# A state-space scan over single positions becomes a scan over blocks of four, with factors made during the feed-forward ahead

## The reference

```python
lam_bar = jnp.exp(lam * dt)                       # 32 groups x 64 complex states
b_bar = ((lam_bar - 1.0) / lam)[:, :, None] * b_mat
bu = jnp.einsum('bsgh,gph->bsgp', uf.astype(jnp.complex64), b_bar)
_, states = lax.associative_scan(combine, (a, bu), axis=1)   # s[t] = lam_bar s[t-1] + bu[t]
y = jnp.real(jnp.einsum('bsgp,ghp->bsgh', states, c_mat))
y = y + uf * d_skip
y = jax.nn.gelu(y) ; y = y * sigmoid(y @ w_glu + b_glu)
```

## Time and profile before

| what | value |
| --- | --- |
| median of three runs | 3577.52 us |
| the profiled execution | 3578.64 us, of it the span 3576.8 us |
| TensorE busy | 3240.0 us, 91% |
| VectorE busy | 1843.5 us, 52% |
| ScalarE busy | 956.0 us, 27% |
| GpSimd busy | 380.7 us, 11% |
| mean granted TensorE clock | 0.945 |

### The profile page before, as it was taken

How to read it: one execution, slowest core, us unless ns; L and a number is a source line. 1 busy time by engine, 2 the same in 40 slices (tenths; PEclk the granted TensorE clock), 3 DMA queues, 4 the chain that set the end, 5 groups by cost and what they waited for, 6 DMA issues and landing times.

```text
span 3576.8 us, 49265 instructions
## 1 busy us (share of the span) xinstructions
PE 3240.0 (91%) x20420; PEld 2597.6 (73%) x20420; DVE 1843.5 (52%) x3234; ACT 956.0 (27%) x1669; POOL 380.7 (11%) x539
## 2 busy tenths in 40 slices
PE   8888899999999988899999999899997657789997
PEld 6556788999999866688887888678884212458886
DVE  2352476457564144257646846443335897453334
ACT  2444222232222144422223222222222001432122
POOL 1020121000000002012100000000000684000000
PEclk9999899999999999999999999999998766899999
DMA  5101011224342201011123534122221000112222
GB/s 184 65 13 42 31 60 53 73 101 165 142 142 95 93 36 36 30 45 60 60 91 119 186 121 161 64 89 94 94 100 42 18 0 0 36 61 103 90 99 72
DMA packets 69445, 283.24 MB, mean 79 GB/s; under 512 B 10297, under 2 KB 10681, under 8 KB 64233
## 3 DMA queue, kind: packets, MB, share of 16 engines
q1 hardware_dynamic: 57880, 230.04, 18.1%
q0 software_dynamic: 11344, 50.07, 3.9%
...
## 4 chain that ended last, share of the span: by engine, by line
PE 83%; DVE 11%; issue 3%; ACT 2%; POOL 1%; DMA 0%; DVEq 0%; ACTq 0%; SPq 0%; POOLq 0%
PE acc L1017 15%; PE acc L1018 15%; PE acc L1019 15%; PE acc L1032 8%; PE acc L1240 5%; PE acc L1241 4%; PE acc L1242 4%; PE acc L1179 3%; PE acc L1283 2%; PE acc L1124 2%; PE acc L1183 2%; PE acc L1097 1%; PE acc L1150 1%; DVE work L1857 1%; DVE mixed L2482 1%
## 5 line engine op out<-in xcount | busy, mean ns | idle before, releaser
L1018 PE MATMUL acc<-normed_r,toep_r 128*128 128x512 f32 (+1 forms) x1824 | 643.5, 353 | 0.0
L1908 DVE TENSOR_TENSOR ring_r<-ring,toep_r 128x1024 fp32r<-128x1024 f32 (+2 forms) x328 | 443.7, 1353 | 325.7 <-ACT toep_r L1519 325.7
L1519 ACT ACTIVATE toep_r<-ring 128x1024 fp32r<-128x1024 f32 (+2 forms) x328 | 379.8, 1159 | 724.8 <-PE acc L1019 724.0
L1018 PEld LDWEIGHTS acc<-normed_r,toep_r 128*128 128x128 f32 x1824 | 345.2, 189 | 45.6 <-issue 0.2
L1017 PE MATMUL acc<-work_r,toep_r 128*128 128x512 f32 (+1 forms) x1024 | 354.7, 346 | 6.5 <-DVE temps_r L1899 6.3
L1019 PE MATMUL acc<-work_r,ring_r 128*128 128x512 f32 (+1 forms) x1024 | 354.9, 347 | 0.0
L1017 PE MATMUL acc<-mixed_r,toep_r 128*128 128x264 f32 (+1 forms) x1056 | 344.1, 326 | 5.0 <-DVE ring_r L1908 4.4
L1019 PE MATMUL acc<-mixed_r,ring_r 128*128 128x264 f32 (+1 forms) x1056 | 339.1, 321 | 0.0
L1017 PE MATMUL acc<-temps_r,toep_r 128*128 128x512 f32 x768 | 306.2, 399 | 24.5 <-DVE normed_r L1894 15.1
L1018 PE MATMUL acc<-work_r,toep_r 128*128 128x512 f32 (+1 forms) x880 | 308.1, 350 | 0.0
L1019 PE MATMUL acc<-temps_r,ring_r 128*128 128x512 f32 x768 | 301.7, 393 | 0.0
...
## 6 DMA issues: line engine op xcount, KB each, us to landing
...
extra<-in_w_ada POOLq DMA_DIRECT2D x18, 1024.0 KB, 5.6
toep<-in_w_ada POOLq DMA_DIRECT2D x18, 1024.0 KB, 5.1
...
```

What stands on the lines that cost most here:

```text
L1018: mm(out, wh, xl[:, a:z], start=False, stop=False)
L1519: A(high(ld), slot(ld), ACT.Copy).then_inc(S["w_high"], 1)
L1908: V.tensor_tensor(low(ld), slot(ld), high(ld), ALU.subtract).then_inc(S["w_low"], 1)
```

## The change

The recurrence is solved over blocks of four positions. TensorE computes per block the local state sum of lam_bar^(3-j) B_bar u over the four positions j (`local_states`): 4 x 2 x 4 products per tile of `u`, with 32 rows of weights and 128 columns each, that read every fourth column of `u`. VectorE rotates, scans 128 blocks per pair with rho^4 and rotates back, for four pairs at a time, and also does the sum and difference that GpSimd did. The output is the state at the end of the block before, times C lam_bar^j for each of the four positions (4 x 2 x 4 products with 32 columns of weights, written to every fourth column), plus a short convolution inside the block: for each lag 0 to 3 one product with a block-diagonal lag kernel Re(C lam_bar^lag B_bar) (`lag_kernels`, `outputs`).

The factors (four turned B_bar tiles with powers of lam_bar, four C tiles, four tiles of waves) are made during `ffn1`: VectorE runs one step `ssm_step(i)` behind each of the 22 pairs, TensorE turns tiles in front of the gate products of pairs 8, 9, 12 and 13, ScalarE copies them and runs the Tanh, Exp and Sin in pairs 1 and 3. GpSimd's queue stores each of the 12 tiles of 128x1024 in a DRAM tensor `ssm_store` and loads them in three transfers when `ffn1` has left their places: the B tiles behind the first down product of the second half, waves and C tiles behind the last. Names: `STAGE` is the pair of staging tiles, `WAVE` cosine and sine, `KD` the lag kernels, `ZO` the rotated-back states. The step sizes' Exp moves in front of `ffn1`'s norm, and `discretise`, `sines` and `cosines` go. The scalars and other small tiles move to other places. The core of the diff, in the order layout, GpSimd, TensorE, ScalarE, VectorE; lines taken out are those of the stage described above and aren't shown:

```diff
 NPAIR = 16
...
+STEP = 4
+MADE_AT, TURN_AT = (6, 7, 10, 11), (8, 9, 12, 13)
+FINE, COARSE = 16, SEQ // STEP // 16
 MODS = 72
...
+BBAR, CRE, CIMN = pair_of(E, 0), pp("c_re"), span(E, 1024, 512)
+FC = [span(E, 1536, 256), span(E, 1792, 256), span(E, 2048, 128), span(E, 2176, 128)]
+FN = span(E, 2304, 256)
+STAGE = [span(toep, y0 + 1024 * i, 1024) for i in range(2)]
+SIDE = pair_of(toep, y0 + 2048)
+ssm_store = nc.dram_tensor("ssm_store", (3 * STEP, P, 1024), F32)
+BT = lambda j, c, q: span(T, 1024 * (STEP - 1 - j) + 512 * c + P * q, P)
+CA = lambda j, c: span(toep, 1024 * (j - 1) + 512 * c, 512)
+WAVE = lambda q, c: span(X, s0 + 1024 * q + 512 * c, 512)
+KD0 = s0 + 4096
+KD = lambda q, lag: span(X, KD0 + 512 * q + P * lag, P)
+MP = [span(Ut, 512 * k, 512) for k in range(4)]
+WS, ZS = pair_of(Ut, 2048), pair_of(Ut, 3072)
+ZO = [pair_of(E, 1536), pair_of(Yt, 4 * L)]
...
+        for n in range(3 * STEP):
+            if n < STEP:
+                pool.wait_ge(S["bt_staged"], 2 * n + 2)
+            else:
+                pool.wait_ge(S["ssm_made"], n - STEP + 1)
+            pool.dma_start(ssm_store[n], STAGE[n % 2]).then_inc(ssm_stored[n % 2], 16)
+        for s in range(2):
+            pool.wait_ge(ssm_stored[s], 8 * 3 * STEP)
+        stored = lambda n: ssm_store[STEP * n:STEP * n + STEP].rearrange("n p c -> p n c")
+        block = lambda t, a: span(t, a, 1024 * STEP).rearrange("p (n c) -> p n c", n=STEP)
+        full(pool, b2["ffn1"]["down"][1][0])
+        pool.dma_start(block(T, 0), stored(0)).then_inc(S["bt_loaded"], 16)
+        full(pool, b2["ffn1"]["down"][1][-1])
+        pool.dma_start(block(X, s0), stored(2)).then_inc(S["waves_loaded"], 16)
+        pool.dma_start(block(toep, 0), stored(1)).then_inc(S["ca_loaded"], 16)
+        nc.gpsimd.memset(span(X, KD0, 2048), 0.0).then_inc(S["kd_cleared"], 1)
...
+                if ssm and i in TURN_AT:
+                    turn_inputs(TURN_AT.index(i))
...
+    def turn_inputs(m):
+        pe.wait_ge(S["ba_ready"], m + 1)
+        if m:
+            pe.wait_ge(S["bt_staged"], 2 * m)
+        x = BBAR if m == 0 else [STAGE[m % 2][:, 512 * c:512 * c + 512] for c in range(2)]
+        for c in range(2):
+            for q in range(4):
+                last = turn(PS[:, 6 + c, P * q:P * q + P], x[c][:, P * q:P * q + P], ident)
+        last.then_inc(S["b_turned"], 1)
...
+        def local_states(q):
+            if q:
+                pe.wait_ge(S["bu_read"], q)
+            for c in range(2):
+                for j in range(STEP):
+                    for i in range(4):
+                        r = slice(32 * i, 32 * i + 32)
+                        last = mm(PS[:, i, P * c:P * c + P], BT(j, c, q)[r, :],
+                                  UF[q][r, META + j:L:STEP], start=j == 0, stop=j == STEP - 1,
+                                  skip_group_check=True)
+            last.then_inc(S["bu_ready"], 1)
+        def lag_kernels():
+            for q in range(4):
+                for i in range(4):
+                    n, r = 4 * q + i, slice(32 * i, 32 * i + 32)
+                    w = [x[:, 32 * n:32 * n + 32] for x in BBAR]
+                    for c in range(2):
+                        mm(PS[r, 6, P * q:P * q + 32], w[c], (CRE, CIMN)[c][:, 32 * n:32 * n + 32],
+                           start=c == 0, stop=c == 1)
+                    for c in range(2):
+                        last = mm(PS[r, 6, P * q + 32:P * q + P].rearrange("p (j c) -> p j c", j=STEP - 1), w[c],
+                                  toep[:, 0:1024 * (STEP - 1)].rearrange("p (j c) -> p j c", j=STEP - 1)
+                                  [:, :, 512 * c + 32 * n:512 * c + 32 * n + 32], start=c == 0, stop=c == 1)
+            last.then_inc(S["k_made"], 1)
+        def outputs(q):
+            y = PS[:, 4 + q % 2, :]
+            y3 = y.rearrange("p (k j) -> p k j", j=STEP)
+            u3 = UF[q][:, META:L].rearrange("p (k j) -> p k j", j=STEP)
+            if q >= 2:
+                pe.wait_ge(S["ssm_y"], q - 1)
+            for lag in range(STEP):
+                mm(y3[:, :, lag:STEP], KD(q, lag), u3[:, :, 0:STEP - lag], start=lag == 0, stop=False,
+                   skip_group_check=True)
+            pe.wait_ge(S["z_ready"], q + 1)
+            for j in range(STEP):
+                for c in range(2):
+                    for i in range(4):
+                        n, r = 4 * q + i, slice(32 * i, 32 * i + 32)
+                        last = mm(y[r, STEP + j:SEQ:STEP], CA(j + 1, c)[:, 32 * n:32 * n + 32],
+                                  ZO[q % 2][c][:, P * i:P * i + P - 1], start=False,
+                                  stop=j == STEP - 1 and c == 1, skip_group_check=True)
+            last.then_inc(S["ssm_out"], 1)
+        pe.wait_ge(S["bt_loaded"], 16)
+        local_states(0)
+        pe.wait_ge(S["ca_loaded"], 16)
+        lag_kernels()
+        pe.wait_ge(S["kd_ready"], 4)
         for q in range(4):
...
+            if q < 3:
+                local_states(q + 1)
+            outputs(q)
...
+    def ssm_step(i):
+        if i == 1:
+            act.wait_ge(S["ssm_args"], 1)
+            A(sc["tanh"], sc["half"], ACT.Tanh).then_inc(S["ssm_tanh"], 1)
+            A(sc["exp"], sc["zr"], ACT.Exp).then_inc(S["ssm_tanh"], 1)
+            for k in ("sin1", "cos1", "sinh"):
+                A(sc[k], sc["a_" + k], ACT.Sin).then_inc(S["ssm_sin"], 1)
+        if i == 3:
+            act.wait_ge(S["ang_ready"], 1)
+            for x in FC:
+                A(x, x, ACT.Sin).then_inc(S["fc_ready"], 1)
+        if i in TURN_AT:
+            m = TURN_AT.index(i)
+            act.wait_ge(S["b_turned"], m + 1)
+            if m >= 2:
+                act.wait_ge(ssm_stored[m % 2], 16 * (m // 2))
+            for c in range(2):
+                A(STAGE[m % 2][:, 512 * c:512 * c + 512], PS[:, 6 + c, :], ACT.Copy).then_inc(S["bt_staged"], 1)
...
+        act.wait_ge(S["params2_loaded"], 32)
+        A(sc["dt"], pp("step"), ACT.Exp).then_inc(S["dt_ready"], 1)
...
+        act.wait_ge(S["kd_cleared"], 1)
+        act.wait_ge(S["k_made"], 1)
+        for i in range(4):
+            r = slice(32 * i, 32 * i + 32)
+            A(X[r, KD0:KD0 + 2048].rearrange("p (q j c) -> p q j c", q=4, j=STEP)[:, :, :, 32 * i:32 * i + 32],
+              PS[r, 6, :].rearrange("p (q j c) -> p q j c", q=4, j=STEP), ACT.Copy).then_inc(S["kd_ready"], 1)
...
+    def ssm_step(i):
 
         tt = lambda o, a, b, op: link(V.tensor_tensor(o, a, b, op))
         ts = lambda o, a, s1, s2, o1, o2=None: link(V.tensor_scalar(o, a, s1, s2, o1, o2) if o2 is not None
                                                     else V.tensor_scalar(o, a, s1, None, o1))
+        if i == 0:
+            arguments(tt, ts)
+        elif i == 1:
+            ts(sc["t2"], sc["theta"], float(STEP), None, ALU.mult)
+            reduced(sc["thq"], sc["t2"], sc["n"])
+            angles(0, FINE, "thq", "fine")
+        elif i == 2:
+            ts(sc["t2"], sc["thq"], float(FINE), None, ALU.mult)
+            reduced(sc["t3"], sc["t2"], sc["n"])
+            angles(1, COARSE, "t3", "coarse")
+            dve.sem_inc(S["ang_ready"], 1)
+        elif i == 3:
+            radii(tt, ts)
+        elif i == 4:
+            factors(tt, ts)
+        elif i == 5:
+            powers(tt)
+        elif i == 6:
+            rotated(BBAR, pairs3(pp("b_re")), pairs3(pp("b_im")), "cr", "ci", S["ba_ready"])
+            link(V.tensor_scalar(CIMN, pp("c_im"), -1.0, None, ALU.mult))
+        elif i in MADE_AT:
+            m = MADE_AT.index(i)
+            if m >= 2:
+                dve.wait_ge(ssm_stored[m % 2], 16 * (m // 2))
+            rotated(stage(m), pairs3(BBAR[0]), pairs3(BBAR[1]), f"p{m}r", f"p{m}i", S["ba_ready"])
+        elif 14 <= i < 14 + STEP:
+            j = i - 13
+            n = STEP + j - 1
+            dve.wait_ge(ssm_stored[n % 2], 16 * (n // 2))
+            rotated(stage(n), pairs3(CRE), pairs3(pp("c_im")), f"p{j}r", f"p{j}i", S["ssm_made"],
+                    conjugate=True)
+        elif 14 + STEP <= i:
+            g = i - 14 - STEP
+            if g == 0:
+                dve.wait_ge(S["fc_ready"], 4)
+            n = 2 * STEP + g
+            dve.wait_ge(ssm_stored[n % 2], 16 * (n // 2))
+            waves(g, n)
...
+    def rotated(out, re, im, pr, pi, signal, conjugate=False):
+        cb = lambda x: sc[x].unsqueeze(2).to_broadcast([P, NPAIR, 32])
+        o, side = [pairs3(x) for x in out], [pairs3(x) for x in SIDE]
+        V.tensor_tensor(o[0], re, cb(pr), ALU.mult)
+        V.tensor_tensor(side[0], im, cb(pi), ALU.mult)
+        V.tensor_tensor(o[1], re, cb(pi), ALU.mult)
+        link(V.tensor_tensor(side[1], im, cb(pr), ALU.mult))
+        V.tensor_tensor(out[0], out[0], SIDE[0], ALU.subtract)
+        if conjugate:
+            last = V.scalar_tensor_tensor(out=out[1], in0=out[1], scalar=-1.0, in1=SIDE[1], op0=ALU.mult,
+                                          op1=ALU.subtract)
+        else:
```

(51 more changed lines are left out.)

224 lines of the change are left out of this document (47 added, 177 removed).

## The result

The changed kernel took 3408.34 us (median of four runs, 3405.15 to 3410.56), the one before 3577.55 (median of four, the three of the time before among them): ratio 0.9527, interval 0.9511 to 0.9544. It is faster by 169.2 us. The forecast was 3434 with a range of 3418 to 3470: the sign and the place of the gain were right, its size was put 25 us too low. The profiled execution took 3410.56, of it the span 3408.8, so 168.1 less than the span of before.

A forecast was written before the change was run, and what follows sets the result against it. TensorE was taken to bound the feed-forward and VectorE the state-space stage. Stage -151.2, transposes +7.2 and table load +0.2 sum to -143.8 us, giving 3434 us, range 3418 to 3470.

The forecast's parts named there:

- What bounds the kernel: TensorE bounds the feed-forward and VectorE the state-space stage; work out of VectorE's stage is time, inside feed-forward gaps free.
- the attention's clock: Attention behind the stage: where the clock rises may shift, -11 to +5 us; taken as 0 in the sum.
- the price of a scan: VectorE in the stage: 0.5 us per 128-wide scan, eight taken as 4.0 a group, bounds 3.4 to 13.4.
- the transposes: TensorE in the feed-forward: four rounds of eight transposes on the path, 7.2 us, upper bound 14.1.
- VectorE per group: Stage: products, sums, scans and back rotation for four pairs take 11.9 us with waits, and VectorE stays the bound.
- Fourfold overlap: TensorE in the stage: records on four row or column groups run together, 1.8 us a group at full clock.
- rival (b): Stage: TensorE's strided SBUF reads and PSUM writes take twice their time; +43 us, 3477; chance 0.10.
- The lag kernels: TensorE at the stage's start: 64 products, 128 records, 7.7 to 20 us, to fit under VectorE's first group.
- stall: VectorE waits after its first group for lag kernels, copies and second local states: 1 to 14 us, taken as 2.
- (a): Stage: TensorE's records overlap only in pairs, so TensorE bounds the stage; +26 us, 3460; chance 0.17.
- (c): Feed-forward: the cover fails, a VectorE or ScalarE step is late each pair; +20 to +45, 3454 to 3479; chance 0.10.
- (d): Stage slower than before: TensorE's products neither overlap nor keep their speed; 3643 us; chance 0.02.

The follow-up runs named there:

- The doubling run: The kernel after with each of the four groups of eight transposes in ffn1 made twice; ffn1 grew from 380.71 to 384.22 us.
- fillers: The kernel after with extra TensorE products into a free bank, before or also within the attention, in three versions: 3420.05, 3418.29 and 3421.46 us.

## Why the prediction was right, and where it was not

**What bounds the kernel: right.** VectorE bounds the new stage without a gap, the feed-forward hides its steps, the gain is the stage. The 24.3 us between the sum's -143.8 and the measured -168.1 are no single error. Two steps failed: the attention's clock, a term put at 0 without a reason, and the price of a scan. In numbers, three terms were mis-sized, all to one side: the attention (6.9), the scans (5.3) and the transposes (3.7). One was in no step, the spacing of the large products (5.0). Chance (1.9) and smaller sizes make up the rest. None of them alone would have left the range.

**VectorE per group: the price of the scans was the step that failed.** I worked out 0.5 us each from the 1.67 of the earlier trace rows, with a fixed share of 0.10. But 1.67 is the mean of a scan of 1.21 and one of 2.21 that waited for GpSimd: alone a scan of 512 takes 1.16 and one of 128 takes 0.33. I had seen this effect for the products, and took their lone price from the earlier trace rows, but did not put the scan under the same doubt. 8 x (0.50 - 0.33) = 1.3 us a group, 5.3 in all. Both bounds stood on the same ground: the lower one, 0.42 a scan by pure proportion, lies above what was measured, so it bounded nothing. Sums (1.32 for 1.35) and back rotation (3.75 for 3.9) were right.

**TensorE in the stage.** Fourfold overlap was right for the state products (1.94 for 1.8) and missed for the local states at the full clock (3.9 for 1.8) because of rival (b)'s reads. Being hidden, they cost only the first one: VectorE began at 2803.6, not 2802.3, while TensorE's first product in the stage came 0.2 later than forecast. The lag kernels were far too dear: 7.7 to 20 forecast, about 3 measured. VectorE's second group started with no stall, where I took 2. ScalarE's copies begin when the lag kernels end, at 2806.39:
```profile
2803.57 2.48 DVE L2582 TENSOR_TENSOR normed<-acc,work 128x512 f32<-128x512 f32 x4 [76.77 <-PE acc L1455]
```
```profile
2806.39 2.42 ACT L1858 ACTIVATE work<-acc 32x512 f32<-32x512 f32 x4 [6.96 <-PE acc L1469]
```
Together: start +1.1, stall -2, four groups -6.4 (41.2 for 47.6), the tail 3.7 for 3.6. The stage lasted 50.3 from its first product for 57.5. Of these 7.2 us the norm and projections ahead gave back 0.6 (85.6 us from the norm to the stage, 85.0 before), which I had at 0; no run tests why.

**Transposes: wrong price.** I read the 0.44 of the earlier trace rows for L1457 as one transpose in two records; it was two transposes, and the earlier trace rows counts them. 32 x 0.11 = 3.5, not 7.2. The doubling run shows it.

**The attention: the largest term, named but put at 0.** -6.9 lies in my -11 to +5. The sum took 0 and gave no reason for 0 rather than a gain: this is the other step that failed. The clock fits it: 41 us at 0.50 before, 29 after, which at half a microsecond each is about 6 of the 6.9. That the changed stage shortens the time at 0.50 is seen in every kernel built on it without fillers, and in the kernel before with GpSimd's work cut (24.2); what sets its length stays open.

**What no step had.** The closer spacing of the large products: 2.1 us in `ffn1`, which grew by 1.4, the 3.5 of its transposes less 2.1, and 2.3 in the second feed-forward, whose part of the span is 2.9 shorter. That is some 5 us in all, cause open. And 1.9 us ahead of `ffn1` are chance.

**The rivals.** (a) did not decide: TensorE was never the bound. (b) was half true, reads but not writes, and VectorE's groups covered it. (c) was wrong: no step held TensorE up, and the last eight cost nothing outside the feed-forward either. (d) never came near. The range stopped at 3418 because the attention (-11), the scans (-3) and the stall (-2) were all the gains that it allowed for. The transposes were bounded only upwards, and the scans from a row with GpSimd at work; what such a row hides is a gain too.
